# Memory stage projections of a two-layer block: float32 products replaced by three single-pass products of high and low parts

## The chip, the cores and the metric

One NeuronCore of one Trainium2 chip runs the whole program. The metric is the device time of one launch in microseconds (us); the median of several launches is compared. TensorE (PE) multiplies, VectorE (DVE) and ScalarE (ACT) work elementwise and empty the PSUM banks, SyncE (SP) issues the loads of weights, GpSimd (POOL) issues a few small ones.

## The reference, cut to what matters

The program computes two transformer-like blocks on 256 tokens of width 1024. The stage in question is the cross attention to a memory of 256 rows, in the middle of the first block:

```python
def memory_cross_attention(h, m, w_q, w_kv, w_o):
    q = (h @ w_q).reshape(B, S, MEM_HEADS, MEM_HEAD_DIM)
    k, v = jnp.split(m @ w_kv, 2, axis=-1)
    ...
    s = jnp.einsum('bqhd,bmhd->bhqm', q, k) * (MEM_HEAD_DIM ** -0.5)
    p = jax.nn.softmax(s, axis=-1)
    o = jnp.einsum('bhqm,bmhd->bqhd', p, v).reshape(B, S, D_MODEL)
    return o @ w_o
# in the block, all in float32, 4 heads of 256:
c = memory_cross_attention(rms_norm(h, mem_pre_norm), rms_norm(mem, mem_kv_norm),
                           mem_w_q, mem_w_kv, mem_w_o)
h = h + rms_norm(c, mem_post_norm)
f = swiglu(rms_norm(h, ffn2_pre_norm), ffn2_w_gate, ffn2_w_up, ffn2_w_down)
```

## The kernel before, in words

The program is a sequence of stages A to F: A is the first feed-forward, B the mixer, C the memory stage, D the second feed-forward, E a hybrid of convolution and attention, F a mixture of experts. Every engine has its own written-out order of instructions, and semaphores tie them together.

Weights stream through a ring of four slots. A slot holds a block of 1024 x 512 numbers as 8 chunks of 128 rows (`wide`) and behind it a tail of 2048 numbers per partition (`down`, used by the feed-forwards). SP loads block b (three transfers, 2 MB together; 3 MB in a feed-forward) as soon as the entry `release[b - 4]` says that PE has left the slot. The memory stage uses ten blocks: 0 and 1 (first half of `mem_w_kv`, for k), 2 (the first 512 columns of v), 3 and 4 (`mem_w_q`), 5 (the last columns of v), 6 and 7 (`w_ada_2`, for a later stage), 8 and 9 (`mem_w_o`).

PE's order in the memory stage (`pe_part`): k features from blocks 0 and 1 (L504 in `pe_features`: 256-column products, the weights stationary), v for two tiles of 128 tokens from block 2 (L490 in `pe_tokens`: 512-column products, the weights moving), the transposes of the normed h (L463), v of tile 0 from block 5 (L1764), q from blocks 3 and 4 (L504), scores (L1783), v of tile 1 from block 5 (L1764), half of the gate product (L867), the transposes of the soft-maxed scores (L1798) around the other half, probabilities times v (L1808), and the output projection from blocks 8 and 9 (L490). The memory's features `memT` and all weights are plain float32.

DVE copies each full bank to SBUF (L1823, L1829), multiplies h's features by a gain (`vec_to_features`, L411), and does the softmax's scaling and maxima. ACT does the exponentials (L1879) and the norms. Ahead of its own output norm each of the two also cuts the first two pieces of stage D's weights (`cut_ahead`, L683 and L690).

The cut is the form that the feed-forwards and part of stage F have already: ACT copies float32 numbers into a float32r tile, `high`; DVE subtracts this from the float32 numbers into another float32r tile, `low`; PE adds up three products, by the pairs

```python
PAIRS = ((0, 0), (0, 1), (1, 0))   # (part of the weights, part of x): low*low is left out
```

In the feed-forward this is L701 and L736 for pieces of 2048 numbers per partition, L664 for 256-column products, L643 for 512-column ones, and L612 and L624 (`act_cut_x`, `vec_cut_x`) for x.

Of the kernel before, what the change touches and what calls it, by code (L numbers as in the profile page):

```python
# [19 lines left out]
F32 = mybir.dt.float32  # L20
F32R = mybir.dt.float32r
I32 = mybir.dt.int32
ALU = mybir.AluOpType
# [105 lines left out]
def program(nc, A, out, ctx):  # L129
# [255 lines left out]

    def vec_residual(v, bank, start, order):

        g = v.gain()
        scaled = view(arena, start, (T, D))
# [12 lines left out]
    def vec_to_features(v, dst, chunks, gain=None, tell=True):  # L402


        for c in range(0, chunks, 2):
            b = v.q.take()
            if gain is None:
                v.do(v.eng.tensor_copy(dst[:, c:c + 2, :], view(ps[b], 0, (2, S))), psum_free)
            else:
                for k in range(2):  # L410
                    v.do(v.eng.tensor_scalar(dst[:, c + k, :], ps[b][:, k * S:(k + 1) * S],  # L411
                                             gain[:, c + k:c + k + 1], None, ALU.mult),
                         psum_free if k else None)
        if tell:
            v.feed()

# [66 lines left out]

    def pe_tokens(pe, lhs, n=512, bias=None):

        w = wide[pe.slot()]
        for t in range(T):
            b = pe.q.fill()
            for c in range(DC):
                ins = pe.eng.matmul(ps[b][:, 0:n], lhs[:, c, t * P:(t + 1) * P], w[:, c, 0:n],  # L490
                                    start=c == 0, stop=c == DC - 1 and bias is None)
            if bias is not None:
                ins = pe.eng.matmul(ps[b][:, 0:n], bias[0], bias[1], start=False, stop=True)
            ins.then_inc(psum_full, 1)
        pe.released()

    def pe_features(pe, rhs):

        w = wide[pe.slot()]
        for f in range(0, 4, 2):  # L500
            b = pe.q.fill()
            for k in range(2):
                for c in range(DC):
                    ins = pe.eng.matmul(ps[b][:, k * S:(k + 1) * S],  # L504
                                        w[:, c, (f + k) * P:(f + k + 1) * P], rhs[:, c, :],
                                        start=c == 0, stop=c == DC - 1)
            ins.then_inc(psum_full, 1)
        pe.released()

    def pe_product(pe, lhs):  # L510

        for _ in range(2):
            pe_tokens(pe, lhs)

    def vec_product_residual(v, start):

        vec_residual(v, lambda t, n: ps[v.hand()], start, BY_HALF)
        v.give_back(4)
# [46 lines left out]
    ff_tmp, ff_end = carve(ff_end, 2, S)  # L565
    addr = {t: nc.lookup_mloc(x).addr for t, x in (("arena", arena), ("xn", xn), ("xT", xT))}

# [28 lines left out]
    def ff_weight_sems(tag):  # L596

        return [[sem(f"{tag}_{x}{p}") for p in range(3)] for x in ("high_set", "low_set")]

    x_high_set = sem("x_high_set")  # L600
# [165 lines left out]
    def dense(tag, gain_at, first, scale, shift):  # L766
# [9 lines left out]
        def vec_part(v):  # L776
            if first:
                v.ask()
                v.ask()
            vec_norm(v, h)  # L780
            if first:
                vec_cut_first(v, tag, base[0], 0)
                v.eng.wait_ge(gains_loaded, 16 * PRE_GAINS)
            vec_cut_x(v, preg[:, gain_at])
            if first:
                vec_cut_first(v, tag, base[0], 1)
            vec_ff(v, tag, NF, base[0])

            vec_residual(v, ff_bank, ff_end + 2 * PIECE, BY_TILE)

# [159 lines left out]
    def mixer():  # L950
# [406 lines left out]
        def vec_part(v):  # L1357
# [204 lines left out]
            for k in range(2):  # L1562
                b = mine.take()
                do(cp(xT[:, 4 + 2 * k:6 + 2 * k, :], view(ps[b], 0, (2, S))), vec_free)
                e.sem_inc(gdn_features, 1)
            vec_product_residual(v, 0)

        def act_part(a):
# [81 lines left out]
            do(f(oss, oss, ACT.Sqrt, bias=eps[:], scale=1.0 / GD))  # L1650
            a.eng.sem_inc(roots_set, 1)
            act_product_norm(a)

        def sp_part(sp):
# [16 lines left out]
    def memory():  # L1671
        MH, HC = 4, 2
        LEFT_OUT = 2
        memT = view(ring[1][:, DC * 512:SLOT], 0, (DC, S))
        oT, e = carve(0, DC, S)
        kT, e = carve(e, DC, S)
        val, e = carve(e, T, D)
# [11 lines left out]
        mem_set, mem_ready = sem("mem_set"), sem("mem_scales_set")  # L1689
        SQUARES, NORMED, FEATURES = 1, 2, 3  # L1690

# [44 lines left out]
        def act_features(a, mine):  # L1736
            for c in range(0, DC, 2):
                b = mine.take()
                for k in range(2):
                    a.do(a.eng.activation(memT[:, c + k, :], ps[b][:, k * S:(k + 1) * S],  # L1740
                                          ACT.Copy, scale=preg[:, 3, c + k:c + k + 1]),
                         mine.free if k else None)
            a.eng.sem_inc(mem_set, 1)

        def sp_rows(sp):
# [4 lines left out]
        def pe_part(pe):  # L1750
            mm, tr = pe.eng.matmul, pe.eng.transpose
            pe.eng.wait_ge(mem_set, FEATURES)
            for _ in range(2):
                pe_features(pe, memT)
            pe_tokens(pe, memT)
            pe_tiles_to_features(pe, strided(xn), DC)
            values_block = pe.block + 2
            pe.eng.wait_ge(loaded[values_block % NS], 16 * LOADS * (values_block // NS + 1))
            w = wide[values_block % NS]

            def last_values(t):
                b = pe.q.fill()
                for c in range(DC):
                    ins = mm(ps[b][:], memT[:, c, t * P:(t + 1) * P], w[:, c, :], start=c == 0,  # L1764
                             stop=c == DC - 1)
                ins.then_inc(psum_full, 1)

            last_values(0)
            pe.get()
            for _ in range(2):  # L1770
                pe_features(pe, xT)
            assert pe.block == values_block
# [4 lines left out]
            for t in range(T):  # L1777
                for hd in range(0, MH, 2):
# [6 lines left out]
                    ins.then_inc(psum_full, 1)  # L1785
            last_values(1)
            release[mine] = (psum_full, pe.q.n)
# [16 lines left out]
            for c in range(0, DC, 2):  # L1804
# [6 lines left out]
                ins.then_inc(psum_full, 1)  # L1811
            pe.get()
            pe.leave_out(LEFT_OUT)
            pe_product(pe, oT)

        def vec_part(v):
            e, do = v.eng, v.do
            vec_norm(v, h)

            def take(dst, n):  # L1820
                for c in range(0, DC, 2):
# [12 lines left out]
            values(0, 1)  # L1834
            take(qT, 4)
            v.feed()
# [22 lines left out]
            for t in range(T):  # L1859
                for hd in range(0, MH, 2):  # L1860
# [8 lines left out]
            v.feed()  # L1869
            v.ask()  # L1870
            cut_ahead["vec"](v)
            vec_product_residual(v, 12288)

        def act_part(a):
            act_norm(a, h)
            a.get()
            for t in range(T):
                for hd in range(MH):
                    a.do(a.eng.activation(soft[:, t, hd, :], soft[:, t, hd, :], ACT.Exp,  # L1879
                                          bias=mx[:, t, hd:hd + 1],  # L1880
                                          accum_out=den[:, t, hd:hd + 1]))
                a.put()
            a.get()
            cut_ahead["act"](a)
            act_product_norm(a)

        def sp_part(sp):
# [7 lines left out]
            for lo in (0, 512):  # L1895
                sp.project("mem_w_o", lo, natural=True)
        ahead = dict(pe_transposes=pe_transposes, vec_scale=vec_scale, act_squares=act_squares,
                     act_scale=act_scale, act_features=act_features, sp_rows=sp_rows)
        return (pe_part, vec_part, act_part, sp_part), ahead
# [1258 lines left out]
```

## Time and profile before

| | |
|---|---|
| median of 3 runs | 1626.22 us (1624.29 to 1627.47) |
| span of the profiled execution, first to last instruction | 1623.4 us |
| mean granted clock of PE over the span | 0.982 of full |
| PE busy over the span | 95% |
| PE busy from 423.9 to 560.1 us (memory stage) | 132.65 of 136.20 us |

The profiled execution has no launch time of its own on record beside its span, so the span stands for it; it is 2.8 us below the median of the other runs. Times in the trace are counted from the span's start. A float32 matmul instruction leaves two records in the trace, so 32 instructions show as x64; a float32r one leaves one.

### The profile page before, as it was taken

To read this page: it belongs to the slowest core of one execution; us is meant where nothing else is said; L and a number is where in the kernel's file an instruction comes from. 1 tells how busy PE (TensorE), PEld (TensorE's weight loads), DVE (VectorE), ACT (ScalarE), POOL (GpSimd) and SP (SyncE) were. 2 spreads that over 40 slices of the span, in tenths; PEclk is the share of its full clock that TensorE was granted. 3 is DMA by queue.
4 is the path that set the end of the run, shared out by engine and by line. 5 is a ranking of instruction groups with operands and counts; after the bars stand their busy time and mean duration, and the time that the engine had idled before them with its cause. 6 is when DMAs were issued, how large, how long until landed. Compare 5 with 4: busy or idle time off the path is not lost.

```text
span 1623.4 us, 26939 instructions
## 1 busy us (share of the span) xinstructions
PE 1541.9 (95%) x10354; PEld 1010.3 (62%) x10354; DVE 700.6 (43%) x1239; ACT 453.2 (28%) x729; POOL 45.9 (3%) x97
## 2 busy tenths in 40 slices
PE   6999999999999899999999999978998999989987
PEld 6999978666666499997854455454434444434442
DVE  5555447345213355555499855461121222222212
ACT  4433343141101343334101253032222222222221
POOL 6000010000000000000100000000000000000000
PEclk9999999999999999999999999979999999999999
DMA  9846392311425736455644423419998997998984
GB/s 320 286 156 205 107 326 107 128 53 53 169 104 187 259 127 205 155 181 199 223 156 156 152 94 120 174 35 367 350 402 298 351 364 240 346 339 295 359 328 171
DMA packets 156214, 350.88 MB, mean 216 GB/s; under 512 B 12655, under 2 KB 57919, under 8 KB 155712
## 3 DMA queue, kind: packets, MB, share of 16 engines
q1 hardware_dynamic: 152464, 343.05, 58.6%
q0 software_dynamic: 1792, 3.09, 0.7%
q10 hardware_dynamic: 1840, 3.17, 0.5%
q8 instruction: 74, 1.21, 0.3%
q14 instruction: 44, 0.36, 0.1%
HBM read 579.89 MB, written 2.16 MB: 359 GB/s over the span
## 4 chain that ended last, share of the span: by engine, by line
PE 42%; DVE 10%; DMA 7%; SPq 3%; ACT 3%; issue 2%; DVEq 0%; ACTq 0%
PE bank L2740 8%; PE bank L664 8%; PE bank L2768 6%; DVE arena L2225 6%; PE bank L2026 5%; DMA ring<-in_w_exp_down 4%; PE bank L643 4%; PE bank L2674 3%; DMA ring<-in_w_exp_gu 3%; PE bank L2654 2%; SPq L2991 2%; PE bank L2017 2%; PE bank L490 2%; ACT arena L2451 1%; SPq L2996 1%
## 5 line engine op out<-in xcount | busy, mean ns | idle before, releaser
L664 PE MATMUL bank<-x_high,w_high 128*128 128x256 f32 x704 | 201.1, 286 | 6.1 <-DVEq L252 6.1
L664 PE MATMUL bank<-x_low,w_high 128*128 128x256 f32 x704 | 200.8, 285 | 0.0
L664 PE MATMUL bank<-x_high,w_low 128*128 128x256 f32 x704 | 199.5, 283 | 0.0
L736 DVE TENSOR_TENSOR w_low<-ring,w_high 128x2048 fp32r<-128x2048 f32 x60 | 137.4, 2293 | 77.2 <-ACT w_high L701 76.9
L2026 PE MATMUL bank<-ring,xT 128*128 128x512 f32 x384 | 166.0, 592 | 1.8 <-ACT arena L2383 1.8
L664 PEld LDWEIGHTS bank<-x_high,w_high 128*128 128x128 f32 x704 | 134.0, 190 | 7.6 <-issue 6.9
L664 PEld LDWEIGHTS bank<-x_high,w_low 128*128 128x128 f32 x704 | 135.6, 193 | 0.0
L664 PEld LDWEIGHTS bank<-x_low,w_high 128*128 128x128 f32 x704 | 134.2, 191 | 0.7
L701 ACT ACTIVATE w_high<-ring 128x2048 fp32r<-128x2048 f32 x60 | 114.6, 1913 | 61.3 <-PE bank L643 59.2
L2026 PEld LDWEIGHTS bank<-ring,xT 128*128 128x128 f32 x384 | 72.6, 190 | 91.9 <-issue 91.8
L2740 PE MATMUL bank<-ring,xn 128*32 128x512 f32 x1024 | 114.9, 593 | 11.9 <-DMA ring<-in_w_exp_gu 10.6
L2768 PE MATMUL bank<-ring,arena 128*32 128x512 f32 x1024 | 117.4, 599 | 6.7 <-DMA ring<-in_w_exp_down 6.7
L2740 PE MATMUL bank<-ring,xT 128*32 128x512 f32 x1024 | 114.3, 593 | 6.1 <-DMA ring<-in_w_exp_gu 6.1
L2920 DVE SCALAR_TENSOR_TENSOR arena<-bank,arena 128x256 f32<-128x256 f32 x32 | 15.5, 484 | 218.5 <-ACT arena L2968 218.5
L2225 DVE SCALAR_TENSOR_TENSOR arena<-arena,sm 128x256 f32<-128x256 f32 x240 | 95.2, 478 | 0.0
L2740 PEld LDWEIGHTS bank<-ring,xn 128*32 128x32 f32 x1024 | 32.4, 110 | 90.9 <-issue 67.6
L2740 PEld LDWEIGHTS bank<-ring,xT 128*32 128x32 f32 x1024 | 32.8, 110 | 84.7 <-issue 70.1
L2930 DVE TENSOR_TENSOR y_low<-bank,y_high 128x512 fp32r<-128x512 f32 x64 | 44.3, 692 | 90.4 <-ACT y_high L2974 90.4
L2968 ACT ACTIVATE arena<-bank 128x256 f32<-128x256 f32 x32 | 12.3, 384 | 221.8 <-PE bank L2740 221.8
L2768 PEld LDWEIGHTS bank<-ring,arena 128*32 128x32 f32 x1024 | 30.7, 111 | 65.9 <-issue 58.8
L1068 PE MATMUL bank<-xT,ring 128*128 128x256 f32 x320 | 70.5, 380 | 0.1
L2974 ACT ACTIVATE y_high<-bank 128x512 fp32r<-128x512 f32 x64 | 38.2, 597 | 104.4 <-PE bank L2768 104.4
(532 smaller groups left out, 2268.1 us busy)
## 6 DMA issues: line engine op xcount, KB each, us to landing
ring<-in_w_exp_gu SPq DMA_DIRECT2D x512, 512.0 KB
ring<-in_w_exp_down SPq DMA_DIRECT2D x128, 1024.0 KB
ring<-in_w_in SPq DMA_DIRECT2D x42, 768.0 KB, 6.1
ring<-in_ffn_w_gate SPq DMA_DIRECT2D x22, 1024.0 KB, 5.5
ring<-in_ffn_w_up SPq DMA_DIRECT2D x22, 1024.0 KB, 8.0
ring<-in_ffn_w_down SPq DMA_DIRECT2D x21, 1024.0 KB, 10.1
ring<-in_w_ada SPq DMA_DIRECT2D x24, 768.0 KB, 5.7
ring<-in_w_in SPq DMA_DIRECT2D x21, 512.0 KB, 7.3
```

The source lines that it names most:

```text
L643: ins = pe.eng.matmul(ff_bank(t, m)[:], ff_h[x][:, a % 2, f, t * P:(t + 1) * P], (last_down if last else ff_w[2])[w][:, f, m * 512:(m + 1) ...
L664: ins = pe.eng.matmul(bank[:, k * S:(k + 1) * S], ff_w[f][w][:, c, k, :], (x_high, x_low)[x][:, c, :], start=c == 0 and i == 0, stop=c == ...
L701: ac.eng.activation(high[:], raw_piece(s, p), ACT.Copy).then_inc(high_set[p], 1)
L736: v.eng.tensor_tensor(low[:], raw_piece((base + a) % NS, p), high[:].bitcast(F32), ALU.subtract).then_inc(low_set[p], 1)
L1068: ins = mm(ps[b][:, k * S:(k + 1) * S], w[:, c, (f + k) * P:(f + k + 1) * P], xT[:, c, :], start=c == 0, stop=c == DC - 1)
L2026: ins = mm(ps[b][:], lhs[:, c, t * P:(t + 1) * P], w[:, c, :], start=c == 0, stop=c == DC - 1 and bias is None)
L2225: ins = stt(acc[:, c, :], src, taps[:, c, i:i + 1], acc[:, c, :], ALU.mult, ALU.add)
L2674: mm(ps[2 * t + n][:], seated[i % 2][:, t * P:(t + 1) * P], part[:, n, :], start=False, stop=False, skip_group_check=True)
L2740: ins = mm(ps[4 + half][SEATS * g:SEATS * (g + 1), :], packed[q % 2][:, c, at:at + SEATS], wide[s][:, c, :], start=c == 0, stop=c == DC - ...
L2768: ins = mm(ps[6 + n][r, :], hidT[:, j, r], down[s][:, j, n * 512:(n + 1) * 512], start=j == 0, stop=j == 1, skip_group_check=True)
L2930: do(tt(y_low[:, n, :], ps[6 + n][:], y_high[:, n, :].bitcast(F32), ALU.subtract), y_low_set)
L2974: do(f(y_high[:, n, :], ps[6 + n][:], ACT.Copy), y_high_set)
```

## The change

The products of all eight projection blocks of the memory stage become three single-pass products of high and low parts. Each block is cut in two halves of 2048 numbers per partition (`Half`), by columns where PE makes features and by rows (chunks) where it makes tokens. The high half goes to one of six places (ring tails and stretches of the arena), the low half over the raw weights in the ring. Three of the places are used again and again, so ACT must wait until PE has left a place (`half.before.left_by`). The first four halves are cut in the mixer's last part, the others between the stage's own work. The memory's features are cut once (`mem_parts`), x by the feed-forward's routine (`act_cut_x`, `vec_cut_x` in place of `vec_to_features`), and the attention's output into `o_high` (ACT) and `o_low` (DVE) in place of the copy by DVE. Scores, transposes and probabilities times v stay as they were. In `tokens` both tiles go through the first half block before the second. The diff, cut to its core:

```diff
+    class Half:
+        def __init__(self, block, cut, k, place, before=None):
+            self.high = high_half(place, cut)
+            self.low = cut(ring_low[block % NS], k)
+            self.before = before
...
+    def pe_half(pe, half):
+        pe.eng.wait_ge(half_low, half.number)
+        return half.high, half.low
+    def act_half(a, half):
+        b = half.block
+        if half.before is not None:
+            a.eng.wait_ge(*half.before.left_by)
+        a.eng.wait_ge(loaded[b % NS], 16 * LOADS * (b // NS + 1))
+        a.eng.activation(half.high, half.cut(wide[b % NS], half.k), ACT.Copy).then_inc(half_high, 1)
+    def vec_half(v, half):
+        v.eng.wait_ge(half_high, half.number)
+        v.eng.tensor_tensor(half.low, half.cut(wide[half.block % NS], half.k),
+                            half.high.bitcast(F32), ALU.subtract).then_inc(half_low, 1)
...
# mixer, vec_part (act_part in the same way, without vec_low)
-            vec_product_residual(v, 0)
+            MEM["vec_low"](v)
+            for half in MEM["halves"](0, 2):
+                vec_half(v, half)
+            vec_product_residual(v, view(arena, 0, (T, D)))
+            for half in MEM["halves"](2, 4):
+                vec_half(v, half)
...
# memory stage, pe_part
+            places = [0, 1, 2, 0, 1, 2, 3, 4, 0, 1, 2, 0, 1, 2, 5, 1]
+            blocks = (0, 1, 2, 5, 3, 4, 8, 9)
...
+            def features(block, parts, fed=False):
+                for half in of[block]:
+                    b = pe.q.fill()
+                    high, low = pe_half(pe, half)
+                    for k in range(2):
+                        for c in range(DC):
+                            ...
+                            for i, (w, x) in enumerate(PAIRS):
+                                ins = mm(ps[b][:, k * S:(k + 1) * S], (high, low)[w][:, c, at],
+                                         parts[x][:, c, :], start=c == i == 0, ...)
+                    half.left_by = (psum_full, pe.q.n)
+            def tokens(block, tiles, parts, feed=lambda c: None):
+                banks = [pe.q.fill() for _ in tiles]
+                for m, half in enumerate(of[block]):
+                    high, low = pe_half(pe, half)
+                    for b, t in zip(banks, tiles):
+                        for c in range(4):
+                            ...
+                    half.left_by = (psum_full, pe.q.n - (0 if m else len(tiles) - 1))
...
# memory stage, vec_part
-            take(kT, 4)
+            take(kT[:, 0:4], 2)
+            cut(4, 6)
+            take(kT[:, 4:8], 2)
+            cut(6, 8)
             values(0, 0)
             values(1, 0)
-            vec_to_features(v, xT, DC, preg[:, 2])
+            vec_cut_x(v, preg[:, 2])
+            cut(8, 10)
             values(0, 1)
+            cut(10, 12)
             take(qT, 4)
...
+            cut(12, 14)
             gate1_part(1)
-            take(oT, 4)
+            for k in range(4):
+                b = v.hand()
+                v.eng.wait_ge(o_high_set, k + 1)
+                do(e.tensor_tensor(o_low[...], view(ps[b], 0, (2, S)), o_high[...], ALU.subtract), psum_free)
+                e.sem_inc(o_low_set, 1)
             v.leave_out(LEFT_OUT)
-            v.feed()
             v.ask()
+            cut(14, 15)
             cut_ahead["vec"](v)
+            cut(15, 16)
...
# memory stage, act_part
             act_norm(a, h)
+            for half in cut_halves[4:8]:
+                act_half(a, half)
+            act_cut_x(a, preg[:, 2])
+            for half in cut_halves[8:12]:
+                act_half(a, half)
             a.get()
             ...   # the exponentials
+            for half in cut_halves[12:15]:
+                act_half(a, half)
+            for k in range(4):
+                a.eng.activation(o_high[...], view(bank, 0, (2, S)), ACT.Copy).then_inc(o_high_set, 1)
             a.get()
             cut_ahead["act"](a)
+            for half in cut_halves[15:16]:
+                act_half(a, half)
             act_product_norm(a)
```

## Rows read from the trace of the kernel before

**Rows 1.** The page: the span and the busy time of each engine.
```profile
span 1623.4 us, 26939 instructions
PE 1541.9 (95%) x10354; PEld 1010.3 (62%) x10354; DVE 700.6 (43%) x1239; ACT 453.2 (28%) x729; POOL 45.9 (3%) x97
```
**Rows 2.** Memory stage by windows: length, busy PE, PEld, DVE, ACT, POOL, clock, DMA.
```profile
423.90:560.10 136.20, 132.65 (x513) 89.01 (x511) 39.11 (x54) 18.18 (x40) 0.95 (x1) 1.00 0.53 183
```
**Rows 3.** Groups by shape, PE, 423.9 to 560.1: count, busy us, mean ns.
```profile
L504 PE MATMUL bank<-ring 128*128 128x256 f32 x128 | 27.8, 379 | 0.0
...
L490 PE MATMUL bank<-ring,arena 128*128 128x512 f32 x64 | 27.7, 593 | 1.2 <-DVEq L252 1.2
...
L1764 PE MATMUL bank<-ring 128*128 128x512 f32 x32 | 14.1, 592 | 0.0
```
**Rows 4.** Chain that ended last, in stage D: start, us, what.
```profile
593.99 5.46 PE bank L643 x24
599.45 11.52 PE bank L664 x96
```
**Rows 5.** The page's groups of cuts, on DVE and ACT: count, busy us, mean ns.
```profile
L736 DVE TENSOR_TENSOR w_low<-ring,w_high 128x2048 fp32r<-128x2048 f32 x60 | 137.4, 2293 | 77.2 <-ACT w_high L701 76.9
...
L701 ACT ACTIVATE w_high<-ring 128x2048 fp32r<-128x2048 f32 x60 | 114.6, 1913 | 61.3 <-PE bank L643 59.2
...
L2930 DVE TENSOR_TENSOR y_low<-bank,y_high 128x512 fp32r<-128x512 f32 x64 | 44.3, 692 | 90.4 <-ACT y_high L2974 90.4
...
L2974 ACT ACTIVATE y_high<-bank 128x512 fp32r<-128x512 f32 x64 | 38.2, 597 | 104.4 <-PE bank L2768 104.4
```
**Rows 6.** Timeline, end of the mixer to q: start, us, instruction [idle before].
```profile
408.53 1.53 DVE L1564 COPY xT<-bank 128x512 f32<-128x512 f32 x2 [7.62 <-PE bank L1349]
...
413.97 0.60 ACT L375 ACTIVATE xn<-bank 128x512 f32<-128x512 f32 x1 [16.11 <-PE bank L1336]
...
424.01 27.79 PE L504 MATMUL bank<-ring 128*128 128x256 f32 x128
...
465.37 1.94 PE L463 MATMUL bank<-ident,xn 128*128 128x128 f32 x16
```
**Rows 7.** Block 5's load: the queue's row, then DMA by windows.
```profile
451.83 1.43 SPq L549 DMA_DIRECT2D ring<-in_mem_w_kv  x3
```
```profile
452.00:453.00 1.00, 1.00 (x4) 0.46 (x3) 0.60 (x1) 0.00 (x0) 0.00 (x0) 1.00 0.10 12
...
459.00:460.00 1.00, 1.00 (x4) 0.50 (x3) 0.46 (x1) 0.00 (x0) 0.00 (x0) 1.00 0.15 55
```
**Rows 8.** Timeline, scores to output projection.
```profile
509.73 7.03 PE L1764 MATMUL bank<-ring 128*128 128x512 f32 x16
...
520.89 2.87 DVE L1862 COPY arena<-bank 128x512 f32<-128x512 f32 x4
...
523.87 7.17 PE L1808 MATMUL bank<-arena 128*128 128x256 f32 x32 [0.79 <-DVEq L252]
...
532.29 27.70 PE L490 MATMUL bank<-ring,arena 128*128 128x512 f32 x64 [1.25 <-DVEq L252]
```
**Rows 9.** Timeline, start of stage D: x is cut.
```profile
569.08 1.00 DVE L624 SCALAR_TENSOR_TENSOR x_low<-bank,preg,x_high 128x256 fp32r<-128x256 f32 x2 [0.22 <-DVE x_low L624]
```
**Rows 10.** Clock: windows (clock third from the end), timeline of PE after its pause.
```profile
559.50:562.50 3.00, 0.50 (x2) 0.00 (x0) 1.63 (x3) 2.20 (x6) 0.00 (x0) 1.00 0.28 78
562.50:572.50 10.00, 7.09 (x32) 6.74 (x33) 6.18 (x13) 6.19 (x15) 0.00 (x0) 0.50 0.83 291
...
318.00:325.00 7.00, 7.00 (x28) 3.41 (x25) 4.07 (x6) 2.06 (x4) 0.00 (x0) 0.76 0.70 265
```
```profile
564.50 3.65 PE L463 MATMUL bank<-ident,xn 128*128 128x128 f32 x16 [4.50 <-DVEq L252]
...
570.27 0.41 PE L664 MATMUL bank<-x_high,w_low 128*128 128x256 f32 x1
...
570.48 0.41 PE L664 MATMUL bank<-x_high,w_high 128*128 128x256 f32 x1
```

More of the change, by code:

```diff
@@ L384, in act_bank_norm, with vec_residual @@
                 a.put()
-    def vec_residual(v, bank, start, order):
+    def vec_residual(v, bank, scaled, order):
         g = v.gain()
-        scaled = view(arena, start, (T, D))
         for t, n in order:
@@ L482, in strided, with vec_product_residual @@
         return lambda c, t: v[:, t, c, :]
[L484 to L517, printed above, removed]
+    def vec_product_residual(v, scaled):
+        vec_residual(v, lambda t, n: ps[v.hand()], scaled, BY_HALF)
         v.give_back(4)
@@ L1651, in act_part @@
             a.eng.sem_inc(roots_set, 1)
+            for half in MEM["halves"](0, 2):
+                act_half(a, half)
             act_product_norm(a)
+            for half in MEM["halves"](2, 4):
+                act_half(a, half)
         def sp_part(sp):
@@ L1674, in memory @@
         memT = view(ring[1][:, DC * 512:SLOT], 0, (DC, S))
+        mem_parts = [ring_tail[i][:].rearrange("p (c s) -> p c s", c=DC) for i in (3, 1)]
         oT, e = carve(0, DC, S)
+        o_high = parts_at("memory_out_high", "arena", 0, DC, S)
+        o_low = [parts_at(f"memory_out_low{k}", "arena", start, DC // 2, S)
+                 for k, start in enumerate((2048, 11264))]
+        PLACES = [ring_tail[0], parts_at("memory_half0", "arena", 12288, HALF), ring_tail[2],
+                  parts_at("memory_half1", "arena", 0, HALF),
+                  parts_at("memory_half2", "arena", 10240, HALF), ring_tail[3]]
+        cut_halves = []
         kT, e = carve(e, DC, S)
@@ L1751, in pe_part @@
             mm, tr = pe.eng.matmul, pe.eng.transpose
[L1752 to L1755, printed above, removed]
+            first = pe.block
+            places = [0, 1, 2, 0, 1, 2, 3, 4, 0, 1, 2, 0, 1, 2, 5, 1]
+            cuts = 2 * [by_columns] * 2 + 4 * [by_rows] + 4 * [by_columns] + 4 * [by_rows]
+            blocks = (0, 1, 2, 5, 3, 4, 8, 9)
+            latest = {}
+            for i, (x, cut) in enumerate(zip(places, cuts)):
+                latest[x] = Half(first + blocks[i // 2], cut, i % 2, PLACES[x], latest.get(x))
+                cut_halves.append(latest[x])
@@ new lines, in pe_part @@
+            of = {block: cut_halves[2 * i:2 * i + 2] for i, block in enumerate(blocks)}
+            def features(block, parts, fed=False):
[4 more added lines that the diff above has]
+                        for c in range(DC):
+                            if fed and k == half.k == c % 2 == 0:
+                                pe.get()
+                            at = slice(k * P, (k + 1) * P)
+                            for i, (w, x) in enumerate(PAIRS):
+                                ins = mm(ps[b][:, k * S:(k + 1) * S], (high, low)[w][:, c, at],
+                                         parts[x][:, c, :], start=c == i == 0,
+                                         stop=c == DC - 1 and i == 2, skip_group_check=True)
+                    ins.then_inc(psum_full, 1)
+                    half.left_by = (psum_full, pe.q.n)
@@ L1756, in pe_part @@
+            mem_part = lambda x, c: mem_parts[x][:, c, :]
+            pe.eng.wait_ge(mem_low_set, 1)
+            for block in range(2):
+                features(block, mem_parts)
+                pe.block += 1
+                pe.released()
+            tokens(2, range(T), mem_part)
+            pe.block += 1
+            pe.released()
             pe_tiles_to_features(pe, strided(xn), DC)
             values_block = pe.block + 2
-            pe.eng.wait_ge(loaded[values_block % NS], 16 * LOADS * (values_block // NS + 1))
@@ L1759, in pe_part @@
[L1759 to L1771, printed above, removed]
+            tokens(5, [0], mem_part)
+            for block in (3, 4):
+                features(block, (x_high, x_low), block == 3)
+                pe.block += 1
+                pe.released()
@@ L1785, in pe_part @@
                     ins.then_inc(psum_full, 1)
-            last_values(1)
+            tokens(5, [1], mem_part)
             release[mine] = (psum_full, pe.q.n)
@@ L1811, in pe_part, with out_part, fed @@
                 ins.then_inc(psum_full, 1)
-            pe.get()
-            pe.leave_out(LEFT_OUT)
-            pe_product(pe, oT)
+            pe.q.n += LEFT_OUT
+            assert pe.block == first + 8
+            def out_part(x, c):
+                return o_low[c // 4][:, c % 4, :] if x else o_high[:, c, :]
+            def fed(c):
+                if c % 2 == 0:
+                    pe.eng.wait_ge(o_low_set, c // 2 + 1)
+                if c == DC - 2:
+                    pe.eng.sem_inc(psum_full, LEFT_OUT)
+            tokens(8, range(T), out_part, fed)
+            pe.block += 1
+            pe.released()
+            tokens(9, range(T), out_part)
+            pe.block += 1
+            pe.released()
         def vec_part(v):
@@ L1818, in vec_part, with cut @@
             vec_norm(v, h)
+            def cut(lo, hi):
+                for half in cut_halves[lo:hi]:
+                    vec_half(v, half)
             def take(dst, n):
-                for c in range(0, DC, 2):
+                for c in range(0, 2 * n, 2):
                     b = v.q.take()
                     do(e.tensor_copy(dst[:, c:c + 2, :], view(ps[b], 0, (2, S))), psum_free)
-            take(kT, 4)
             def values(t, n):
@@ L1882, in act_part @@
                 a.put()
+            for half in cut_halves[12:15]:
+                act_half(a, half)
+            for k in range(4):
+                bank = a.full(a.hand())
+                a.eng.activation(o_high[:, 2 * k:2 * k + 2, :], view(bank, 0, (2, S)), ACT.Copy)\
+                 .then_inc(o_high_set, 1)
             a.get()
             cut_ahead["act"](a)
+            for half in cut_halves[15:16]:
+                act_half(a, half)
             act_product_norm(a)
```

62 lines of the change are left out of this document (45 added, 17 removed).

## The prediction, made before the changed kernel was run

> **What bounds the kernel now.** I read the page first, for the engine with the largest busy share: PE is busy for 95% of the span [rows 1]. A share over the whole span says nothing of one stage, so the windows of the memory stage come next. From 423.9 to 560.1 us PE is busy for 132.65 of 136.20 us at full clock, DVE for 39.11 and ACT for 18.18 [rows 2]. So the stage ends when PE has got through its list, and two engines have room. Then the groups by shape, for what a product costs. "Mean ns" includes overlap, so I take the pitch, busy time over count. 256 columns in float32: 27.8 / 128 records = 0.217 us, two records per instruction, 0.434. 512 columns: 27.7 / 64 = 0.433, so 0.866 per instruction [rows 3]. Last the chain in stage D, where the three-product form already runs: 11.52 / 96 = 0.120 us for 256 columns, 5.46 / 24 = 0.228 for 512 [rows 4].
>
> **The products.** Three of them cost 0.360 against 0.434, and 0.684 against 0.866. The four feature blocks have 32 instructions each, the four token blocks 16 each. A feature block goes from 13.9 to 11.52 us, 4 x 2.38 = 9.5 saved. A token block goes from 13.9 to 10.95, 4 x 2.95 = 11.8 saved. Together 21.3 us of PE, if nothing makes PE wait.
>
> The Trainium skill, TensorE: Matmul & The Clock Gate, section "Back-to-back issue gap", gives columns / 2.4 + 2.5 ns, so 109 and 216 ns. With these figures the products would save 384 x 11 ns and 192 x 12 ns more, some 6.5 us. The trace does not agree: with a new stationary operand before most products the pitch is 120 and 228 ns [rows 4], and the sum above goes by that.
>
> **Not on the path.** Tile 1 of block 5 runs in 7.03 us at 509.7 while DVE and ACT do the softmax [rows 8]. The next thing that ends late there is the softmax, not PE: probabilities times v starts 13.98 us after the scores' end, on DVE's copies at 520.89 + 2.87 [rows 8]. Its 1.55 us of saving (7.03 - 5.48) goes nowhere. Left: 19.7.
>
> **A wait removed.** Output projection starts at 532.29, 1.25 us after probabilities times v end, as it waits for the last copy [rows 8]. Now PE needs only the first of four `o_low` to start and the third and fourth for the second half block. ACT's o_high (0.6) and DVE's o_low (0.69) [rows 5] follow each bank, the last about 1.5 us behind PE. DVE first cuts halves 12 and 13 after its last softmax copy, 2 x 2.29, and copies the gate part, 0.72: ready 5.3 us after 13.9, before PE's 7.17 us [rows 8] are up. ACT has to make half 14 before the first o_high; its block is released with tile 1 of block 5 (5.5 us after the scores) and lands about 7.4 later (below), plus 1.9 is 15 us after the scores; the first bank is there at 15.8. Gain 1.2. Sum 20.9.
>
> **The cuts.** A half costs ACT 1.91 and DVE 2.29 [rows 5], which I took at 1.88 and 2.25 to 2.29; sixteen halves are 31 us of ACT and 37 of DVE. I walked through all three orders. PE starts at 424.01 as before [rows 6]. The memory's low part and halves 0 and 1 need DVE for 6.9 us from 410.1, the end of its last copy of features [rows 6], and are done at 417, before the last three output banks of the mixer; ACT had 16.11 us of idle before the first of them [rows 6]. So they cost nothing; without that idle time they would cost up to 6.9. Halves 2 to 5 wait on ACT for PE to leave a place (429.8, 435.6, 441.4), but PE works 5.76 us on a feature half, and 1.9 + 2.3 + 0.2 = 4.4 us after a place is left the new half is there; PE wants it one or two halves later. The norm of h comes behind half 3 on ACT's queue, about 6.3 us later than now, and ends at 437, where its transposes are wanted at 458. Blocks 0, 1 and 2 end at 435.5, 447.0 and 458.0.
>
> Block 5 is the first place that is tight. It can be loaded only when block 1 is left, at 447.0. The trace has its issue at 451.83 and the last data at about 459.2, 7.4 us [rows 7]. So it lands at 454.6; ACT's half 6 is there at 456.5, DVE's at 458.8, half 7's at 461.1. PE ends the transposes (1.94 [rows 6]) at 459.9 and tile 0 of block 5 (5.48) at 465.4. No wait yet. But on DVE's queue two copies of v (2.87 / 4 = 0.72 each [rows 8]), then the cut of x stand before half 8. That cut costs 4 x 1.22 - 0.22 = 4.7 us (1.00 per bank plus 0.22 [rows 9]). So DVE is at 462.5 after the copies, 467.3 after x, and half 8 is ready at 469.6. PE stands from 465.4 to 469.8: **4.4 us of stall**, where the kernel before had none. After that, half 11 (place left at 475.6) is ready at 479.9, wanted at 487, and q ends at 492.8 instead of 501.8. In the output projection half 12 is ready at 517 and half 15 (place left at 530.2, behind the two cuts for stage D) at 534.5, wanted at 538.5. Sum 20.9 - 4.4 = 16.5; handing over between engines at 16 new waits I set at 0.4 in total from the 0.1 us pieces of the existing ones. 16.1 at full clock.
>
> **The clock.** After the output projection PE pauses for 4.50 us; the clock is full until 562.5, then 0.50 for 10 us [rows 10]. Products of 256 columns then start 0.21 us apart [rows 10] against 0.120. My new pause is as long as that one, so I expect the clock to fall. How long for: at 318 to 325 us 0.76 over 7 us, i.e. 3.4 us at the lower level; after 562.5, 10 us [rows 10]. Each busy us at the lower level loses 1 - 0.120/0.213 = 0.44. If it falls 3 us into the pause, 1.4 us of it are in the pause: a loss of 0.9 (2.0 x 0.44, for 3.4 us) to 3.8 (8.6 x 0.44, for 10). I take 2.2, since neither row is nearer: the pause is that of the long one, the work behind it is dense as in the short one. The Trainium skill, same page, section "HAM oscillation — how this bites in real kernels", says that idle gaps of this kind put PE back to half rate each time they occur. By that rule the price is due; the trace agrees at 562.5.
>
> Forecast: 16.1 - 2.2 = 13.9 us. Span 1623.4 - 13.9 = 1609.5; the median stands 2.8 above the span, so 1626.2 - 13.9 = **1612.3 us**. Stages D to F start earlier by this and do the same work, expert loads are issued in answer to PE, so the gain stays.
>
> **Rivals.**
> 1. No stall: block 5 lands earlier or DVE goes quicker. For it: DVE has to make up only 4.4 us in 35. Against: the queue order is fixed and each duration is a row. Gain 20.5, time 1605.7. Chance 0.10.
> 2. The cuts are exposed at more places: loads land in 10 us rather than 7.4 (block 9's with stage D's 3 MB behind it), or SBUF traffic of ACT, DVE and PE together stretches the cuts. One more stall of 4.4 with a fall of clock (2 to 4) and 2 us on the first: 16.1 - 2.2 - 4.4 - 3.5 - 2 = 4, time 1622, at mild values 1618. For it: every half from 2 on hangs on a place being left. Against: L736 and L701 were measured beside busy PE. Chance 0.16, of it 0.04 within 0.2%.
> 3. Slower: the clock, once down in the pause at 468, stays down. At 0.44 lost per busy us it takes 16.1 / 0.44 = 37 us at the lower level to eat the gain; through q, scores, v and output projection (about 62 us of PE at full clock) it would add some 48, 1658 us. For it: three short products per float32 one suffer the same factor. Against: the longest low stretch in the rows is 10 us. Chance 0.03.
> 4. The form isn't faster here, since the low half is written over the ring with a stride: 0.434 again. Within 0.2%. Chance 0.02.
>
> The forecast (stall of 3 to 6 us, with or without the clock's fall: gain 11 to 17.5) has 0.69. 0.2% is 3.3 us, about what a measurement tells from no change. Faster 0.69 + 0.10 + 0.12 = 0.91; same 0.04 + 0.02 = 0.06, slower 0.03. The range leaves out rival 3 and the ends of 1 and 2: 1607.5 to 1618.
>
> **What would show it.** In the trace after: feature products 0.120 apart and token ones 0.228; first products of block 0 at 424; one pause of PE of 4 to 5 us just before q, ended by DVE's low half, with DVE's queue showing two copies, x and one cut before it; the granted clock at 0.50 right after; q ending at 493 to 497; no pause before the output projection; the end of it 12 to 16 us sooner than 560.0; stage D on as before. I am wrong if PE's pause is elsewhere, if halves 2 to 5 come late (ACT waiting for places), or if stage D's first cuts wait for their load.

## The result, and the profile after

The changed kernel has a median of 1618.84 us (7 runs, 1611.18 to 1621.42) beside 1625.76 us before (7 runs); the ratio is 0.9949, 95% interval 0.9935 to 0.9964. The same kernel was timed again later, 20 launches in all with a median of 1616.0, against 47 of the kernel before with 1625.05. (One further launch of the kernel before took 4822.6 us and is left out.) So it is 7 to 9 us faster, where 13.9 had been forecast, and the first median stands just above the stated range of 1607.5 to 1618. The profiled execution has the very span that was forecast, 1609.5. That is luck: it is the fastest of the seven launches, and the sum below shows that errors cancel in it.

The page after, the span and the engines' busy time:

```profile
span 1609.5 us, 27392 instructions
...
PE 1522.5 (95%) x10546; PEld 1020.3 (63%) x10546; DVE 738.6 (46%) x1256; ACT 489.8 (30%) x758; POOL 45.7 (3%) x97
```

Against [rows 1] PE has 19 us less, DVE 38 and ACT 37 more: the products' saving and the cuts, both by the prediction's sums (21.3 saved less what the lower clock gives back; 37 and 31 for sixteen halves and the rest for x, the memory and the output). Next the chain through the stage (start, us, what), from the mixer's last product:

```profile
407.51 14.00 PE bank L1341 x32
421.51 22.93 PE bank L1803 x192
444.46 0.37 SPq L502
444.88 0.49 SPq L502
445.41 8.04 DMA ring<-in_mem_w_kv
453.47 1.93 ACT memory_half L596
455.49 2.30 DVE ring_low L602
457.79 0.14 issue
457.93 5.83 PE bank L1820 x24
...
466.01 2.53 issue
468.54 24.62 PE bank L1803 x192
...
515.21 7.17 PE bank L1879 x32
522.38 22.31 PE bank L1820 x96
...
546.41 1.29 DVE h L396
```

(L502 issues loads, L596 and L602 are ACT's high and DVE's low part of a cut, L1803 and L1820 are the products of features and of tokens, L1879 is probabilities times v.) Blocks 0 and 1 take 22.93 / 2 = 11.5 us each, as 96 x 0.120 says, against 13.9 [rows 3]; the output projection takes 22.31 against 27.70 [rows 8] and follows the probabilities' product without a gap. Between them the chain leaves PE: it runs through the load of the last v block and its cut. A measure free of what comes earlier is the stretch from the end of the mixer's last product (here 421.51) to the start of the last update of h (546.41): 124.90 us, against 561.72 - 424.17 = 137.55 before. I call it the stage's length below; 12.65 us are won in it. The span adds up with three more terms: the stage starts 2.7 us earlier than before, stages D and E take 0.5 us less, and the experts' stage (F) takes 1.9 us more; 12.65 + 2.7 + 0.5 - 1.9 is, rounding aside, the 13.9 of the span.

What the two engines do in the gap, DVE's timeline first, then PE's:

```profile
455.49 4.49 DVE L602 TENSOR_TENSOR ring_low<-ring,memory_half 128x2048 fp32r<-128x2048 f32 x2 [10.26 <-ACT memory_half L596]
459.90 1.41 DVE L1917 COPY arena<-bank 128x512 f32<-128x512 f32 x2
461.34 1.00 DVE L629 SCALAR_TENSOR_TENSOR x_low<-bank,preg,x_high 128x256 fp32r<-128x256 f32 x2
...
464.99 1.00 DVE L629 SCALAR_TENSOR_TENSOR x_low<-bank,preg,x_high 128x256 fp32r<-128x256 f32 x2 [0.21 <-DVE x_low L629]
466.14 2.29 DVE L602 TENSOR_TENSOR ring_low<-ring,ring_tail 128x2048 fp32r<-128x2048 f32 x1
```

```profile
457.93 0.70 PE L1820 MATMUL bank<-memory_half,ring_tail 128*128 128x512 f32 x2 [0.68 <-DVE ring_low L602]
...
468.54 0.55 PE L1803 MATMUL bank<-x_high,ring_tail 128*128 128x256 f32 x1 [4.78 <-issue]
```

DVE does, without a gap, the two cuts of the last v block, two copies of v, the four pairs of x and the cut of q's first half; PE stands for 4.78 us until this is done. The wait is put down to "issue", but 466.14 + 2.29 = 468.43 shows who was waited for: where a wait has no releaser, look for what ended just before it. Ahead of it DVE had been idle for 10.26 us. The clock in the windows around the pause (third number from the end):

```profile
457.00:463.70 6.70, 6.02 (x27) 4.48 (x25) 6.21 (x8) 6.70 (x12) 0.00 (x0) 1.00 0.81 299
463.70:468.50 4.80, 0.05 (x1) 0.00 (x0) 4.29 (x6) 1.79 (x1) 0.00 (x0) 0.99 0.00 0
468.50:472.00 3.50, 3.46 (x17) 3.50 (x18) 3.46 (x3) 0.00 (x0) 0.00 (x0) 0.53 0.00 0
472.00:475.00 3.00, 3.00 (x28) 3.00 (x27) 1.56 (x1) 0.00 (x0) 0.00 (x0) 1.00 0.00 0
```

It fell at the end of the pause, about 4.5 us after PE had stopped, and was back 3.4 us later; 17 products in the first 3.5 us stand against 28 in the next 3.0.

### The profile page after: what moved, and what is told of

It is laid out like the page before. It is cut to its first block, busy times and chain, and to the rows that moved or that the text cites. A ratio compares the mean times of both kernels' runs of the same rounds, so it can differ in the third digit from the quotient of the medians.

```text
span 1609.5 us, 27392 instructions
## 1 busy us (share of the span) xinstructions
PE 1522.5 (95%) x10546; PEld 1020.3 (63%) x10546; DVE 738.6 (46%) x1256; ACT 489.8 (30%) x758; POOL 45.7 (3%) x97
## 3 DMA queue, kind: packets, MB, share of 16 engines
q8 instruction: 76, 1.25, 0.3%
## 4 chain that ended last, share of the span: by engine, by line
PE 69%; DVE 12%; DMA 9%; SPq 4%; ACT 3%; issue 2%; DVEq 0%; ACTq 0%
PE bank L669 16%; PE bank L2857 8%; PE bank L648 7%; DVE arena L2342 6%; PE bank L2885 6%; PE bank L2143 5%; PE bank L1073 4%; DMA ring<-in_w_exp_down 4%; DMA ring<-in_w_exp_gu 3%; PE bank L1803 3%; PE bank L2791 3%; SPq L3108 2%; PE bank L2771 2%; PE bank L1082 2%; PE bank L1820 2%
```

## The experiments

There are twelve runs in three lots: seven edits (one of them twice), the changed kernel three more times, and one more profile of the kernel before. For each I give the timed median and, from its trace, the stage's length and the clock. The stage's length repeats far better than a launch: 137.55 and 137.59 in two profiles of the kernel before, 124.90, 124.93, 124.94 and 125.03 in four of the changed one. Where a change works in this stage, that is the number to read.

**The changed kernel again (e1, e7, e12).** No edit.

> The changed kernel again, unaltered. Its seven times lie in two groups: 1611.2 and 1612.2 us (mean clock 0.984) and five from 1616.0 to 1621.4 (0.980). Theory: the pause of PE of 4.8 us ahead of q (463.8 to 468.5 in the profiled run) makes the clock fall, for 3.4 us in a good run and for about 10 us in a poor one, so that the runs of 0.980 lose some 3 to 7 us more; median 1612 to 1620, and a profile of a run with 0.980 shows a lower level after about 467 us that lasts longer than 3.4 us. Rival: the two groups come from other stages (a fall before 420 us, or loads of the experts), and a profile of either group shows the same 3.4 us after the pause.

> The changed kernel unaltered, for one more profile. If the clock falls by chance after the pause for one, two or three of the trace's 3.4 us steps, this one may show another length than the 3.4 us of the two profiles so far: 1611 us with 3.4 us, up to 3 us more with 10 us. If the launch is one of those near 1617, its trace shows where the 5 us are: in the load of the last v block by theory A of the run beside it, in the experts' loads by rival B.

> The changed kernel unaltered, on the same chip as the filled pause and the early cut, for the comparison: 1616 to 1618 by its earlier medians of 1618.8 and 1617.2; 125.5 us from the start of the memory stage's products to the last update of h if the clock falls for 3.4 us, 127 if for 6.8.

Medians 1617.2 (e1, 6 runs) and 1613.4 (e12, 6 runs); the single launch e7 took 1614.7. All four traces of this kernel have the pause of 4.8 us and the fall of 3.4 us behind it, and the stage takes the same. So the theory of e1 is wrong for these launches, and what differs between them lies elsewhere: the spans 1609.5, 1611.3, 1613.0 and 1610.5 follow the stage's start (421.5, 425.7, 421.8, 421.5) and the experts' stage, which takes 566.9, 564.4, 569.7 and 567.9 us from the last update of h in stage E to the last one of all.

The start follows the clock in the mixer. From 310 to 350 us, with PE busy for 39 us or more of the 40, the mean granted clock is 1.00 in the first trace and 0.91 in e1 (third number from the end):

```profile
310.00:350.00 40.00, 39.02 (x359) 22.80 (x357) 18.97 (x32) 20.67 (x48) 2.51 (x2) 1.00 0.31 107
```

```profile
310.00:350.00 40.00, 39.65 (x272) 21.04 (x272) 17.02 (x28) 17.26 (x41) 2.50 (x2) 0.91 0.28 95
```

From the last update of h in stage A to the mixer's last product it takes 213.0 to 215.5 us in the eight profiles with 0.91 there, both of the kernel before among them, and 211.5 to 212.1 in the six with 0.96 or more. Why the clock falls there in some launches is open. None of the profiled launches of this kernel was above 1615, so where such a launch loses its time no trace shows.

**Cut q's first block early (e2).** DVE and ACT stand idle for 10 us and more while they wait for the load of the last v block. In that time the halves of block 3 (q's first) are cut.

```diff
-            places = [0, 1, 2, 0, 1, 2, 3, 4, 0, 1, 2, 0, 1, 2, 5, 1]
-            blocks = (0, 1, 2, 5, 3, 4, 8, 9)
+            places = [0, 1, 2, 0, 1, 2, 0, 3, 1, 4, 2, 0, 1, 2, 5, 1]
+            blocks = (0, 1, 2, 3, 5, 4, 8, 9)
...
             values(1, 0)
-            vec_cut_x(v, preg[:, 2])
             cut(8, 10)
+            vec_cut_x(v, preg[:, 2])
# ACT: cut_halves[4:10] ahead of act_cut_x, [10:12] behind it; the list of cuts by columns and rows in the new order
```

> The two halves of the first q block are cut before those of the last v block, in the time in which DVE (445.2 to 455.5) and ACT (440.6 to 453.5) wait for the last v block's load; one half takes another place for it. Nothing else changes. Theory that DVE's queue (two cuts, two copies, x, one more cut) makes the pause: PE goes from tile 0 of the last v block to q with under 0.5 us between them, 4.8 us are won, and as there is no pause the clock stays full, 1.5 us or more on top: 6 to 9 us faster than the changed kernel on the same chip, near 1605 in good runs, and its times no longer lie in two groups. Rival, that PE waits for the load or for x and not for the cut of q's weights: the pause stays at 4 us or more and the time is within 1 us. Rival, that the clock's fall comes from something else: 4.8 us and no more, clock below full near 465 us still.

Median 1610.9 (5 runs), 6.3 under e1 in the same lot; stage 120.03 us, 4.9 shorter than the changed kernel's. The 4.8 us pause is gone; up to the end of q one of PE's waits remains, ahead of the last v block (engine, waited for: us, times, longest):

```profile
PE bank L1821 <- DVE ring_low L602: 1.5, 1, 1.5
```

The clock stayed full there, but fell for 3.4 us at 507, behind the softmax, where it had not fallen before:

```profile
507.00:510.50 3.50, 3.50 (x20) 1.54 (x22) 3.23 (x5) 2.19 (x3) 0.00 (x0) 0.53 1.04 386
```

At q's end this kernel is 5.7 us ahead; probabilities times v then starts 14.8 us after the scores' end instead of 14.0. That is why 4.9 and not 5.7 us were won in the stage. So x and the load are not what PE had waited for ahead of q.

**The same with a copy moved (e9, e13).** On DVE, `values(1, 0)` goes between the two cuts of the last v block.

> The early cut of q's first block once more, with the second copy of v between the two cuts of the last v block rather than ahead of both. In the trace of the early cut DVE stood at that copy (456.5) when the raw weights' high part was already there. Theory: the pause of PE ahead of the last v block shrinks from 1.5 to about 0.8 us, the kernel is 0.7 us faster than the early cut, near 1610, within what a measurement tells. Rival, that this pause is set by the load and not by DVE: no change at all in the pause.

> The early cut of q's first block with the copy of v between, again: 1606.0 was its median before. Theory that its two pauses of 1 us or less keep the clock: below 1609.5, at least 6 us under the changed kernel on the same chip. Rival, that 1606.0 was luck: 1610 to 1612, like the first early cut.

```profile
PE bank L1821 <- DVE ring_low L602: 1.0, 1, 1.0
```

The pause went from 1.5 to 1.0 us, the clock did not fall in the stage, and the stage takes 118.85 and 118.83, 1.2 us less than in e2. Medians 1606.0 and 1607.3 (11 launches together: 1602.3 to 1611.3), ratio to the kernel before 0.9887 (0.9866 to 0.9907) and 0.9893 (0.9873 to 0.9913). This version beats both kernels: 18.8 and 17.6 us under the kernel before in their lots, and e13 6.1 under the changed one in the same lot (e12; 10 under the median of all its 20 launches), with the same instructions in another order. The stage explains those 6.1 us. It does not explain the 4.9 and 3.6 us between these medians and e2's, of which it has 1.2; the rest is open.

**One of q's halves ahead of x (e3).**

```diff
-            vec_cut_x(v, preg[:, 2])
-            cut(8, 10)
+            cut(8, 9)
+            vec_cut_x(v, preg[:, 2])
+            cut(9, 10)
```

> Only on DVE: the first half of q's weights is cut ahead of x, the second behind it. By the durations seen: ACT makes the high part by 462, DVE the low part by 464.3, the first piece of x by 465.3; PE's pause shrinks from 4.8 to about 1.6 us, then PE goes at the pace of the cut of x. Theory: 2 to 3 us are won by the shorter pause, and the clock stays full after a pause of 1.6 us (as before the change, where pauses of 1.5 us had no fall behind them), which gives another 1.5 us or more: 3 to 6 us faster. Rival, that the length of the pause doesn't matter for the clock: it still falls, and only 2 to 3 us are won.

Median 1611.7 (6 runs), 5.5 under e1; stage 121.98: 2.9 us shorter. PE's waits there are of at most 1.7 us and sum up to 2.3, and the clock is 1.00 in the windows behind them:

```profile
463.00:467.00 4.00, 2.31 (x12) 1.64 (x11) 3.59 (x4) 3.65 (x3) 0.00 (x0) 1.00 0.13 48
467.00:475.00 8.00, 7.35 (x57) 6.74 (x56) 7.28 (x9) 0.97 (x1) 0.00 (x0) 1.00 0.01 2
```

2.5 us less waiting and 1.5 for the clock (e11 below) make 4.0; the missing 1.0 lies in q, which PE begins at the pace of x's cut, with four short waits. So both ends of the expectation hold: a shorter pause, and no fall behind one of 1.7 us.

**Fill the pause (e11).** Eighteen products of no use, so that PE is busy while it waits.

```diff
                     b = pe.q.fill()
+                    if fed and half.k == 0:
+                        for i in range(18):
+                            mm(ps[b][:], mem_parts[0][:, 0, 0:P],
+                               mem_parts[0][:, 2 * (i % 4):2 * (i % 4) + 2, :],
+                               start=True, stop=True, skip_group_check=True)
                     high, low = pe_half(pe, half)
```

> The changed kernel with 18 products of 512 columns (18 x 0.228 = 4.1 us) put into PE's pause ahead of q, into the bank that q's first half block then starts afresh, so that the result is untouched. DVE's queue, and with it the start of q 4.8 us after tile 0 of the last v block, stays. Theory, that the clock's fall after the pause is a cost of its own: granted clock 1.00 from 464 to 475 us, the memory stage 1.5 to 3 us shorter (3.4 or 6.8 us at the lower level, at 0.44 lost per us), the timed median 2 to 4 us under the changed kernel's. Rival, that the clock's fall costs nothing as the products behind it wait for x anyway: same time within 1 us.

```profile
464.00:475.00 11.00, 10.36 (x58) 8.69 (x57) 10.00 (x13) 4.85 (x3) 0.00 (x0) 1.00 0.17 64
```

```profile
466.92 4.28 PE L1798 MATMUL bank<-ring_tail 128*128 128x512 f32 x18
471.84 0.39 PE L1808 MATMUL bank<-x_high,ring_tail 128*128 128x256 f32 x1 [0.64 <-DVE ring_low L602]
```

q starts as late as before, the clock is full all through, and the stage takes 123.49: 1.45 us less. That is the price of a fall of 3.4 us by itself (3.4 x 0.44 = 1.5). The timed median does not show it, 1616.7 against 1613.4 in the same lot; in this profile the experts' stage took 570.7 us, 2.8 more than in e12, and the mixer 3.4 more, with its clock at 0.91. The first theory holds for the stage, its number for the whole launch does not.

**Output projection in float32 (e5).** Blocks 8 and 9 and the copy of the output as before the change; no halves 12 to 15.

```diff
-            tokens(8, range(T), out_part, fed)
-            tokens(9, range(T), out_part)
+            pe.get()
+            pe.leave_out(LEFT_OUT)
+            # 2 blocks x 2 tiles x 8 products of oT with the raw weights, in float32
# DVE: take(oT, 4) instead of o_low and cut(12, 16); ACT: no halves 12 to 15, no o_high
```

> The output projection (both blocks of mem_w_o) goes back to plain float32 products of the raw weights and a copied output, as before the change; everything ahead of it stays changed. Theory, that PE's own time sets the end of the stage: it gives back 27.7 - 21.9 = 5.8 us and the wait of 1.2 us, so 7.0 us slower than the changed kernel. Rival, that the cuts beside it cost about what they save (ACT and DVE late for the norm or for stage D's first cuts): 0 to 3 us slower.

Median 1624.1 (12 runs), 6.9 above the changed kernel's 1617.2 in the same lot. The projection takes its old 27.7 us again, behind its old wait:

```profile
527.70 27.71 PE L1890 MATMUL bank<-ring,arena 128*128 128x512 f32 x64 [1.25 <-DVEq L252]
```

27.71 - 22.31 = 5.4 and 1.25 make 6.65; the stage took 132.84, 7.9 more. The remaining 1.2 are the clock: after the same pause it stayed low twice as long here.

```profile
469.00:472.00 3.00, 0.53 (x2) 0.56 (x3) 2.92 (x2) 0.00 (x0) 0.00 (x0) 0.76 0.00 0
472.00:475.00 3.00, 3.00 (x16) 3.00 (x15) 2.96 (x3) 0.00 (x0) 0.00 (x0) 0.50 0.00 0
475.00:478.00 3.00, 3.00 (x19) 3.00 (x18) 1.50 (x1) 0.00 (x0) 0.00 (x0) 0.61 0.00 0
478.00:481.00 3.00, 3.00 (x28) 3.00 (x27) 0.00 (x0) 0.92 (x1) 0.00 (x0) 1.00 0.02 5
```

**Two products beside the softmax (e4).** Leaves out the product of low weights with high x in tile 1 of the last v block.

```diff
-            tokens(5, [1], mem_part)
+            tokens(5, [1], mem_part, pairs=PAIRS[:2])
```

> The changed kernel with the third product (low weights times high x) left out in tile 1 of the last v block alone, which runs beside the softmax: 8 products of 0.228 us, 1.8 us less for PE there. Theory, that the softmax's chain on DVE and ACT ends later than PE: no change (within 1 us), PE's idle time ahead of the transposes of the soft-maxed scores longer by 1.8 us. Rival, that PE sets the end there too: 1.8 us faster.

Median 1617.3 (8 runs): no gain, though 1.8 us of PE's work are gone. PE's waits for the soft-maxed scores grew from 1.6 to 3.6 us, as the theory says:

```profile
PE bank L1870 <- DVEq L252: 3.6, 2, 2.0
```

The stage even became longer, 128.17, and the clock fell beside those waits:

```profile
511.00:513.00 2.00, 0.55 (x5) 0.55 (x6) 1.82 (x3) 1.90 (x7) 0.00 (x0) 1.00 1.03 388
513.00:515.00 2.00, 0.55 (x6) 0.31 (x3) 1.54 (x3) 1.82 (x3) 0.00 (x0) 0.86 1.00 369
515.00:517.00 2.00, 1.85 (x8) 1.57 (x8) 1.79 (x4) 2.00 (x2) 0.00 (x0) 0.50 1.05 393
```

It also fell for 6.8 us after the pause ahead of q, as in e5, which makes q 1.2 us longer; the other 2.0 come behind the scores. So the 3.2 us are two longer or new falls, and this run alone can't say what the edit would do at an unchanged clock.

**The last v block after q (e10).** Halves in the order of blocks 3, 4, 5; PE does tile 0 of block 5 after q; DVE copies q ahead of it.

```diff
-            tokens(5, [0], mem_part)
             for block in (3, 4):
                 features(block, (x_high, x_low), block == 3)
                 ...
+            tokens(5, [0], mem_part)
# cut: places, the order of the blocks, cut(8, 12) and values(0, 1) behind take(qT, 4) on DVE
```

> Tile 0 of the last v block is computed after q instead of ahead of it, its halves are cut last, the first q block's halves early. The load of the last v block, 9.0 us from issue to the start of its cut in the changed kernel's trace, then has over 20 us of cover, and the copy of q's last bank lies beside PE's products. PE waits for the cut of x instead: 2 us after the transposes, then at the pace of 1.22 us per two chunks against 0.72, some 3.5 us in all. Theory A, that the timed launches of the changed kernel (near 1617) are slower than the profiled ones (1611 to 1613) because that load lands later in them: here timed and profiled launches agree within 2 us, near 1609 to 1611. Rival B, that the difference lies in stages D to F or in the clock: timed launches are 4 to 6 us above the profiled one here too.

Median 1611.0 (6 runs), stage 119.56, PE's waits for x 2.2 us in four pieces. The profiled launch took 1605.0, the others 1610.7 to 1613.0: six above it, though the load has over 20 us of cover. So theory A does not hold here: launches still differ by six where a late load of the last v block can't matter.

**The kernel before, a second profile (e14).**

> The kernel before, for one more profile: whether its stages take the same times as in the first profile (memory stage 137.7 us from its first product to the last update of h, experts 565 us). If the experts' stage takes 567 us as in the mean of the profiles of the changed kernels, nothing is given back there; if 565 again, some 2 us of the gain may be.

Stage 137.59, experts' stage 565.5 after 565.0. In the twelve profiles of kernels with the change it takes 563.5 to 570.7, 567.3 in the mean.

## Why the prediction was right, and where not

The traces bear out the mechanism in the stage. The forecast of the launch is borne out less well: 6.9 us in the first median, 9.0 over all launches, where a gain of 11 to 17.5 had a chance of 0.69. The ratio 0.9949 on 1626.2 gives 1617.9, just inside the range of 1607.5 to 1618.

- **PE bounds the stage, products of 0.120 and 0.228 us.** Right: 11.5 us per feature block, 22.31 for the output's two blocks (0.232 per product). Undoing one part (e5) gave back 5.4 us of products and the wait of 1.25, where the sum has 5.9 and 1.2. The prediction quoted the formula of the Trainium skill, TensorE: Matmul & The Clock Gate, section "Back-to-back issue gap", by which 6.5 us more would be won. The trace doesn't agree, here too: 120 and 232 ns against 109 and 216.
- **Tile 1 of the last v block saves nothing.** Right: probabilities times v starts 13.96 us after the scores' end (501.25 to 515.21), against 13.98 before, though tile 1 takes 1.1 us less; PE's wait ahead of the transposes went from 0.5 to 1.6. In e4 it grew again by the work left out.
- **The wait ahead of the output projection goes.** Right: 515.21 + 7.17 = 522.38, and there the projection starts; e5 has the 1.25 us back.
- **The cuts elsewhere cost nothing.** Right for halves 0 to 5 and 9 to 15: the trace has no wait of PE for them.
- **The pause ahead of q, and its reason.** Right, 4.78 against 4.4 us, on the same queue in the same order; e2, e3 and e9 show that the order on DVE makes it. Mis-sized was the landing of the last v block, taken as 7.4 us after the first issue. ACT starts its cut 453.47 - 444.46 = 9.0 us after it. The view of transfers has the landing of the third of the three, before and after (the last number, from its own issue, which comes 0.95 us behind the first):

```profile
ring<-in_mem_w_kv SPq DMA_DIRECT2D x1, 512.0 KB, 7.4
```

```profile
ring<-in_mem_w_kv SPq DMA_DIRECT2D x1, 512.0 KB, 8.0
```

So the load had taken 8.3 us in the kernel before as well: the window from 459 to 460 in [rows 7] still has data, and 459.2 was read too early. The other 0.7 us is that the transfer takes longer in the changed kernel; why is not shown. This cost a second pause, 0.68 us ahead of tile 0, which the prediction had at none, and q starts 47.0 us after the stage's start instead of 45.8.
- **The clock.** Right that it falls; its price was taken as 2.2. It is 1.45 for the fall of 3.4 us in the four profiles of the changed kernel (e11 shows it alone), and about 2.7 where the clock stays low for 6.8 us (q takes 25.7 us in e4 and e5 and 22.9 at full clock in e9). The 2.2 was a choice between 0.9 and 3.8, not a reading.
- **The stage's sum.** 13.9 forecast, 12.65 measured: 0.4 for the pause, 0.7 for the second, 0.4 for the output's products, less 0.7 for the clock, explain 0.8 of the 1.25; the rest is not resolved.
- **"The gain stays".** This step failed in part. The four profiled launches of the changed kernel have spans of 1611.1 in the mean against 1623.9 for the two of before, 12.8 less: 12.6 in the stage, 1.6 by an earlier start of it, 0.6 in stages D and E (491.8 to 492.1 us against 492.4 and 492.6), and 2.0 lost in the experts' stage (567.2 against 565.2). All 20 launches together are 9.0 lower in the median. The sixteen that were not profiled take 1616.6 in the mean, the four profiled ones 1612.8. Two stretches outside the change are seen to vary between launches, the experts' stage by 7 us and the mixer by 4, and either could hold the difference. But two profiles of the kernel before are too few to show a lasting loss, and the launches near 1618 were never profiled. So it stays open where they lose 4 us more than the profiled ones.

Of the rivals, a clock that stays down did not come about, and of more exposed cuts there is only the second pause of 0.7 us. At its mild values that rival had 1618, where the first median fell, but the traces don't have its stalls. A kernel without the stall exists (e9), and at 1606 to 1607 it is near where the rival without a stall had put it, 1605.7, though with another order.

## What to carry to other kernels

When work for a saturated engine is paid for with work on others, walk through their queues in order: by their busy time alone all sixteen cuts had cover, and the one that hurt stood behind a load, two copies and x, with 10 us of idle time just before that load was there. Cut what is already there before what is still to land. Judge such a change by the stage's length in the trace, which repeats to 0.1 us here as long as the clock's falls do, and not by launches that scatter by 10; and count a pause of a few us twice, once for itself and once for the clock behind it.

## What the hardware showed that I had not expected

- A pause of 4.8 us was followed by 3.4 us at the lower clock in four profiles and by 6.8 in two, with the same instructions around it. A pause of 1.7 us ahead of dense work (e3) had no fall behind it.
- Less work for PE may bring the clock down elsewhere: with 1.8 us of products left out beside the softmax (e4) it fell there for 6.8 us, and with q ready earlier (e2) for 3.4, though not in e9 and e13 with nearly the same order. One profile each does not show that the edits are the cause.
- The clock also fell in the mixer with PE busy for 39 us or more of 40: 0.91 in the mean of 310 to 350 us in eight of fourteen profiles, and there the mixer took 1 to 4 us longer.
- The third transfer of the last v block's load landed 7.2 and 7.4 us after its issue in the two profiles of the kernel before, and 8.0 to 8.3 in the four of the changed one.
- Filling a pause with useless products keeps the clock full and wins 1.45 us in the stage.
